# One loop for the state-space and mLSTM steps, the decay matrix made by ScalarE, and gate blocks ahead of the branches' transposes

## The reference

```python
# SSD: 8 heads of 64, 2 groups of 4 heads, state 64; a = dt * A, cumulative sum a_cum within the chunk
decay_states = jnp.exp(a_cum[..., -1:] - a_cum)
states = jnp.einsum('bcqgn,bgrcq,bcqgrp->bcgrpn', Bc, decay_states, xc)
Lmat = jnp.exp(segsum(ac))        # exp(a_cum[q] - a_cum[s]) for s <= q, else 0
y_diag = jnp.einsum('bcqgn,bcsgn,bgrcqs,bcsgrp->bcqgrp', Cc, Bc, Lmat, xc)
y_off = jnp.einsum('bcqgn,bcgrpn,bgrcq->bcqgrp', Cc, start_states, jnp.exp(a_cum))
# mLSTM: 4 heads of 128, b = cumulative sum of the log forget gate, m0 the running maximum
Dm = jnp.where(tril, b[..., :, None] - b[..., None, :] + ic[..., None, :], -jnp.inf)
m_t = jnp.maximum(b + m0[..., None], jnp.max(Dm, axis=-1))
s = jnp.einsum('bcqhd,bcshd->bhcqs', qc, kc) * jnp.exp(Dm - m_t[..., None])
num = s @ vc + (qc @ C0) * w_inter
den = jnp.sum(s, axis=-1) + w_inter * (qc @ n0)
h = num / jnp.maximum(jnp.abs(den), jnp.exp(-m_t))
# merge
out = jnp.sum(sigmoid(gate_pre) * proj, axis=2) @ w_out
```

## Time and profile before

| | |
|---|---|
| median of 3 runs | 4205.56 us (4199.91 to 4212.05) |
| the profiled execution | 4204.44 us, span 4202.7 us |
| PE busy | 3844.1 us (91%) |
| DVE busy | 2863.1 us (68%) |
| ACT busy | 1994.6 us (47%) |
| both loops to the first gate block, layer 0 | 366.8 to 633.1 us from the span's start |
| the same, layer 1 | 2983.4 to 3149.0 us |

### The profile page before, as it was taken

How to read it: one execution, slowest core, us unless ns; L and a number is a source line. 1 busy time by engine, 2 the same in 40 slices (tenths; PEclk the granted TensorE clock), 3 DMA queues, 4 the chain that set the end, 5 groups by cost and what they waited for, 6 DMA issues and landing times. The chain is left out here.

```text
span 4202.7 us, 61275 instructions
## 1 busy us (share of the span) xinstructions
PE 3844.1 (91%) x22686; PEld 3257.1 (78%) x22686; DVE 2863.1 (68%) x5816; ACT 1994.6 (47%) x4063; POOL 0.2 (0%) x4
## 2 busy tenths in 40 slices
PE   7999749989999999999999999989759899977998
PEld 4884547778887689999997788868449788867887
DVE  2535564348986868888768766654565499888666
ACT  2243213236666755555556544434224466665443
POOL 0000000000000000000000000000000000000000
PEclk9999869999999999999999999989769999999999
DMA  4221202225564455565554466523005355622665
GB/s 169 72 71 60 98 0 84 100 86 180 183 184 138 135 165 182 184 185 184 183 183 131 140 190 190 161 88 117 0 0 183 119 182 182 186 82 86 189 189 165
DMA packets 142200, 568.35 MB, mean 135 GB/s; under 512 B 15808, under 2 KB 17344, under 8 KB 130240
## 3 DMA queue, kind: packets, MB, share of 16 engines
q1 hardware_dynamic: 142016, 566.14, 42.7%
HBM read 565.03 MB, written 1.05 MB: 135 GB/s over the span
## 5 line engine op out<-in xcount | busy, mean ns | idle before, releaser
L1081 ACT ACTIVATE high<-ring 128x512 fp32r<-128x512 f32 x1632 | 1028.3, 632 | 1031.1 <-PE ps L515 510.1
L1538 DVE TENSOR_TENSOR low<-ring,high 128x512 fp32r<-128x512 f32 x1632 | 1075.8, 688 | 294.1 <-ACT high L1081 282.9
L515 PE MATMUL ps<-h_pair,high 128*128 128x512 f32 x3456 | 1236.1, 400 | 31.7 <-DVE low L1538 30.9
L515 PE MATMUL ps<-h_pair,low 128*128 128x256 f32 x3456 | 970.7, 281 | 0.0
L515 PEld LDWEIGHTS ps<-h_pair,high 128*128 128x128 f32 x3456 | 652.4, 189 | 188.0 <-issue 12.7
L911 PE MATMUL ps<-wt,high 128*128 128x512 f32 x2048 | 713.1, 392 | 5.7 <-DVE low L1538 5.7
L515 PEld LDWEIGHTS ps<-h_pair,low 128*128 128x128 f32 x3456 | 655.4, 190 | 0.0
L913 PE MATMUL ps<-wt,low 128*128 128x256 f32 x2048 | 574.7, 281 | 0.0
L515 PE MATMUL ps<-arena 128*128 128x128 f32 (+8 forms) x2432 | 444.3, 340 | 125.4 <-ACT arena L1081 75.6
L1081 ACT ACTIVATE arena<-ps 128x256 f32<-128x256 f32 (+3 forms) x654 | 271.1, 425 | 514.8 <-PE ps L515 486.1
L515 PEld LDWEIGHTS ps<-arena 128*128 128x128 f32 (+2 forms) x2432 | 326.3, 211 | 218.8 <-issue 115.7
(11 more groups left out here) (171 smaller groups left out, 4442.2 us busy)
## 6 DMA issues: line engine op xcount, KB each, us to landing
ring<-u_in SPq DMA_DIRECT2D x384, 512.0 KB, 3.6
ring<-v_in SPq DMA_DIRECT2D x384, 512.0 KB, 3.6
ring<-win_in SPq DMA_DIRECT2D x56, 1024.0 KB, 4.8
ring<-wmod_in SPq DMA_DIRECT2D x24, 1024.0 KB, 5.0
ring<-wq_in SPq DMA_DIRECT2D x48, 512.0 KB, 3.6
ring<-wmod_in SPq DMA_DIRECT2D x48, 512.0 KB, 3.6
ring<-wbr_in SPq DMA_DIRECT2D x16, 768.0 KB, 4.2
ring<-wout_in SPq DMA_DIRECT2D x8, 1024.0 KB, 4.8
```

The lines of the kernel that those rows point to most:

```text
L515: return pe.matmul(o, l_, r, start=first, stop=last)
L1081: return act.activation(o, i_, f, **kw_)
L1538: return dve.tensor_tensor(o, a, b, op)
```

## The change

1. **One loop.** The SSD step and the mLSTM step of the same chunk and direction run in one step, on all engines. The mLSTM output gets its own `ml_acc`, the SSD scratch its own place behind the mLSTM scratch; `br_high`, `w_high`, `mergedT` move to other addresses.
2. **The decay matrix by ACT.** ACT reads the row sums from PSUM: `Relu(cm - row)` four times for each group, then `Exp(-x)`; `dmat` has a buffer for each group. The mask moves to `cb`, which DVE now multiplies by a triangle instead of copying. `mmat` is gone: the product is written over `dmat`.
3. **Fewer instructions.** The maximum is subtracted in ACT's exponential (four instructions with a bias in place of one), so DVE's subtraction over 512 columns goes; the 4-wide instructions are rearranged (a shown and kept step has seven, before eleven, besides the three of the denominator); the SSD state is made on 128 partitions at once, from two matmuls of 256 columns in place of one of 512; in direction 1 four fused instructions replace a multiplication and an addition.
4. **The order after the loop.** The first gate slot is split and its two gate blocks run before the SSD branch's transposes, the second slot's before the mLSTM branch's.

```diff
+                                for j in range(4):
+                                    h = d * 8 + g * 4 + j
+                                    i = fn(dmat[:, g, j * P:(j + 1) * P], b[:, j * P:(j + 1) * P], ACT.Relu,
+                                           scale=-1.0, bias=cm[:, t, h:h + 1])
+                                i.then_inc(*inc("ssd_row_read", l, d, t, g))
                             for g in range(2):
                                 act.wait_ge(*at("ssd_row_read", l, d, t, g))
...
+                                fn(dmat[:, g, :], dmat[:, g, :], ACT.Exp, scale=-1.0).then_inc(*inc("ssd_L", l, d, t, g))
+                            shown_before = d, t
+                            late_row(MOD_FIRST + 2 * (d * NT + n))
                             act.wait_ge(*at("ml_d", l, d, t))
-                            fn(rW, rD, ACT.Exp).then_inc(*inc("ml_w", l, d, t))
+                            for h in range(MH):
+                                i = fn(rW[:, h * P:(h + 1) * P], rD[:, h * P:(h + 1) * P], ACT.Exp,
+                                       bias=sml[:, 0, 1, h:h + 1])
+                            i.then_inc(*inc("ml_w", l, d, t))
```

```diff
-                                for j in range(4):
-                                    h = d * 8 + g * 4 + j
-                                    i = dve.scalar_tensor_tensor(out=dmat[:, j * P:(j + 1) * P],
-                                                                 in0=b[:, j * P:(j + 1) * P],
-                                                                 scalar=cm[:, t, h:h + 1], in1=nmask[d],
-                                                                 op0=ALU.subtract, op1=ALU.add)
...
+                                tt(cb[:, g * P:(g + 1) * P], b[:, 0:P], tri[d], ALU.mult
+                                   ).then_inc(*inc("ssd_cb_read", l, d, t, g))
...
+                                d3 = dmat[:, g, :].rearrange("p (a b) -> p a b", a=4)
+                                tt(d3, d3, rep(cb[:, g * P:(g + 1) * P], 4), ALU.mult
+                                   ).then_inc(*inc("ssd_m", l, d, t, g))
```

```diff
                             i.then_inc(*inc("gate", l, pr, 2 * q + j))
                         n += 1
+                        if pr == 0 and q == 0:
+                            turn_out("ssd_T", "ssd_norm", acc)
+                        if pr == 0 and q == 1:
+                            turn_out("ml_T", "ml_norm", ml_acc)
```

More of the change, by code:

```diff
@@ L1356, in _ @@
[L1356 to L1360 removed]
+                            b = bank("ml_wT", l, d, t)
+                            fn(rWT, b[:, :], ACT.Copy).then_inc(*inc("ml_wT_read", l, d, t))
+                            late_row(MOD_FIRST + 2 * (d * NT + n) + 1)
+                act.wait_ge(*at("ssd_y_read", l, 1, ORDER[1][-1]))
@@ L1763, in _ @@
-                            first = d == 0
-                            if first:
+                        b = bank("ml_row", l, d, t)
+                        rows = b[:, :].rearrange("p (a b) -> p a b", a=4)
+                        if kept_on:
+                            i = dve.tensor_reduce(mloc, rows, AX.X, ALU.max)
+                        if shown:
+                            i = tt(rD3, rows, rep(nmask[1 - d], 4), ALU.add)
+                        i.then_inc(*inc("ml_row_read", l, d, t))
```

431 lines of the change are left out of this document (198 added, 233 removed).

## The result

The changed kernel takes 4013.32 us (median of four runs, 4005.83 to 4016.44) beside 4203.24 us of the kernel before in the same session: a ratio of 0.9539, with a 95% interval of 0.952 to 0.9559. The profiled execution took 4005.83 us for 4204.44, so 198.6 us less where the prediction had 171.5. The direction and the mechanism were forecast; the profiled gain is larger by 27 us. The profiled execution is the fastest of the four, 7.5 us under their median, so of the 27 us only about 21 are in the medians.

A forecast was written before the change was run, and what follows sets the result against it. It took each loop as a chain passing between engines; merged, layer 0 is bound by DVE's chain (20.0 us) just above TensorE (19.1). Terms -94 - 11.5 - 61 - 5 = -171.5 us from 4204.4 gave 4034 us, range 4012 to 4088.

The forecast's parts named there:

- the work of DVE: DVE instructions in the merged loops: 11.7 us on layer 0's chain, 16.4 us in layer 1's shown, kept step.
- TensorE in a merged step, 19.1: Layer 0's merged loop: TensorE's matmuls and transposes in one step sum to 19.1 us.
- The chain that remains, 20.0: Layer 0's merged step: 7.9 us on TensorE, then 11.7 on DVE, with handovers 20.0; 20.4 in direction 1.
- The bank as its cause: Layer 0: SSD output shares a PSUM bank with the mLSTM's product, so TensorE's output waits until DVE has made `rW`.
- The 4022: Low end of the forecast's own range: TensorE's 19.1 us as layer 0's only bound and layer 1 at 86 us.
- ACT, costed at nothing: Merged loops: ACT's eight `Relu` (2.1 us) and four-part exponential (1.06 for 0.62) are hidden and add no time.
- the 0.7 us ahead of `rW`: Cover for ACT in a shown step: `rW` wants the mLSTM's exponential 0.7 us after it is done.
- Layer 1, 91: Layer 1's merged loop, both directions: 91 us for 152.1, a gain of 61 us; bounds 86 and 99.
- the waits of 3.6 us: Layer 1's shown, kept step: 3.6 us added to DVE's 16.4 for row sums and numerator, making 20.
- The order after the loop, -11.5 and -5: Gate slots behind the loops: the new order saves 11.5 us in layer 0 and 5 in layer 1.
- The fifth rival: Merged loops: steps add up as before, only middle stage and tails go, 36 us: 4169 us; chance 0.03.
- The third: Merged loops: TensorE waits more and falls to the low clock for part of each step: 4082 us; chance 0.17.

The follow-up runs named there:

- Experiment 4: Changed kernel with DVE waiting after each instruction of the merged loop that had no wait behind it: 4034.27 us, ratio 0.9593.
- experiment 2: Changed kernel with the decay matrix's min(row - cm, 0) built by DVE in place of ACT's eight Relu: 4034.96 us, ratio 0.9601.
- experiment 11: Changed kernel with the maximum subtracted by DVE again and ACT's exponential in one piece: 4020.19 us in one run.
- experiment 7: Kernel of Experiment 4 with TensorE's mLSTM carried share issued behind the SSD output instead of ahead of it: 4031.85 us in one run.
- experiment 8: Changed kernel with `kw` made by ACT in four scaled copies in place of one DVE instruction: 4018.2 us, ratio 0.9555.
- experiment 6: Changed kernel with the first gate slot's split moved into the last step of the loop: 4008.21 us, ratio 0.9542.
- experiment 12: Changed kernel with 18 matmuls that nobody reads put into TensorE's wait ahead of the first gate block: 4019.71 us in one run.
- experiment 1: Changed kernel with SSD steps and mLSTM steps in two separate loops again, all else as changed: 4116.93 us, ratio 0.9783.
- experiment 3: Changed kernel with six of the eight matmuls left out of each modulation row in layer 0's loop: 3986.55 us in one run.

## Why the prediction was right, and where it was not

The mechanism held: merging fills each branch's waits with the other's work, and the order behind the loops gave close to what was forecast. What failed is the size of one term, the work of DVE. It was priced as if each instruction had a wait behind it, and with waits for TensorE in layer 1 that mostly did not come. The term stands in both sums: layer 0's chain of 20.0, and layer 1's 91 us, which missed by most.

- **TensorE in a merged step, 19.1.** Measured 18.5; the state, carried shares and output were sized 0.7 too high. That TensorE is the bound of layer 0 was one of the two answers the prediction gave.
- **The chain that remains, 20.0.** This is the step that failed for layer 0. Its 11.7 us of DVE work took 10.6, since 0.72 was taken for each 512-wide instruction and 1.4 for four of 129, the spacing with a wait behind them. Experiment 4 puts the waits back and gives 11.8 and steps of 19.6 to 20.05. So the 20 falls just below 18.5, TensorE becomes the bound, the four middle steps are 1.5 to 1.8 us shorter than forecast and the four others 0.5 to 1: the 9.5 us. The mechanism (DVE's chain a few tenths from TensorE's step) held: 2.3 us put into it cost 2.1 in a middle step where the clock stayed up (experiment 2), 0.7 us cost 2.9 in the loop (experiment 11). The bank as its cause is worth little (0.4 us net, experiment 7). The 4022 that the prediction gives for TensorE as the only bound does not follow from its terms: 4.4 us less in layer 0 and 5 in layer 1 give about 4025; the measured time lies below either.
- **ACT, costed at nothing.** Right in what it cost, not in the cover: the 0.7 us ahead of `rW` was gone in five of layer 0's eight steps, and DVE waited up to 1.94 us for ACT. It showed in no step, because TensorE was the bound. On DVE the decay matrix costs 25 us in both loops, some 4.4 of them by the clock; the rule of the Trainium skill (ScalarE: Activation LUTs, Rules for kernel authors) to use VectorE for relu, which the prediction named, would have been the worse choice here. The cover is small for more: `kw` on ACT has none (experiment 8).
- **Layer 1, 91.** This is the step that failed most: measured 77.3. A shown and kept step took 15.7 (2874.97 to 2890.65 on DVE) for 20, a step not shown 4.6 to 5.5 for 6.1, the last 13.2 and 12.4 for 13.4. Experiment 4 gives 8.3 of the 14 us back. The other 5 to 6 are the waits of 3.6 us that were added to each shown and kept step, of which 0.9 came: the row sums had been costed at half clock, and in that step they ran at full clock. That the last steps' waits of 2.2 came so near (2.7 in direction 0) is in part luck: the numerator stood in the low clock behind TensorE's wait of 1.9 us.
- **The order after the loop, -11.5 and -5.** Measured -10.0 and -5.8. The wait of 3 us before the SSD transposes did not come, because the first slot began at the low clock and ended 15.7 us behind the loop, when the norms had been done for 0.8 us; experiments 6 and 12 take that clock away in layer 0, and in 6 the wait of 2.96 us appears.
- **The fifth rival** (only middle and tails, 36 us) fell with experiment 1. **The third** (low clock in the loop) did not happen in layer 0, where TensorE has no such waits. It did in the last steps of both directions of layer 1, behind waits of 1.9 and 1.7 us, and makes the 0.84 there. Its price is real where such waits are put in (experiments 2, 3, 7).
- **Ahead of the loops** the changed kernel was 4.35 us earlier with nothing changed. In the 14 profiles the loop begins either at 361.0 to 362.6 us (eight of them) or at 365.8 to 366.8 (six, the kernel before among them), and kernels with the same code ahead of it show both. It is no effect of the change. The two groups differ in the granted clock between 100 and 150 us, 0.86 in all eight and 0.80 in all six, and TensorE is busy throughout that window in the changed kernel's profile and in that of before; 50 us at 0.86 would be 53.8 at 0.80, most of the difference (an estimate). What sets the clock there stays open.

## What to carry to other kernels

Take a DVE instruction's price from rows of its own kind of neighbour: with a wait behind it or without. When two bounds of a step lie within a few tenths, an engine's idle time is no slack: count what ends it, and price an edit by the chain. Price a pause of TensorE of 1.5 us or more with a risk: where the clock fell behind it, it cost about its own length again, or more, and in some steps nothing. Put work into it that is there anyway.

## What was not expected of the hardware

- DVE starts 512-column fp32 instructions 0.60 to 0.61 us apart when none has a wait behind it and 0.72 to 0.73 with one; four of 129 columns take 1.13 us, and 1.25 with a wait half-way; two of 128 columns take 0.48 and, with a wait behind each, 0.62.
- Behind most pauses of 1.6 to 4.8 us TensorE's granted clock fell to 0.50 for some microseconds (1.2 for 2.4 GHz), behind 2.38 us at once, behind 1.62 only at the transposes after the output. The length doesn't settle it: behind 1.67, 1.96 and 2.20 us in experiment 2's direction 1 and 2.96 us in experiment 6 it stayed at 1.00, and behind 1.33 us in experiment 4 it fell. In the changed kernel, pauses of 0.92 and 1.4 us at full clock did nothing. Matmuls of no use in the pause kept the clock, in both places where that was tried.
